# The last quarter of the second token tile's residual sum computed on GpSimd

## The reference, cut to what matters

```python
def rms_norm_2(x, g):
    xf = x.astype(jnp.float32)
    y = xf * lax.rsqrt(jnp.mean(xf * xf, axis=-1, keepdims=True) + RMS_EPS)
    return (y * g.astype(jnp.float32)).astype(x.dtype)

def odd_layer(...):
    ...
    y = jnp.concatenate([y_c, y_d], axis=-1) @ w_out
    return x + rms_norm_2(y, g_post)
```

## Time and profile before

| what | us |
|---|---|
| three runs | 812.29, 813.22, 813.26 |
| their median | 813.22 |
| the profiled execution | 811.32 |
| its span, first to last instruction | 809.6 |
| TensorE busy in it | 798.8 (99%) |
| VectorE busy | 509.2 (63%) |
| ScalarE busy | 478.3 (59%) |
| GpSimd busy | 47.4 (6%) |

### The profile page before, as it was taken

How to read it: one execution, slowest core, us unless ns; L and a number is a source line. 1 busy time by engine, 2 the same in 40 slices (tenths; PEclk the granted TensorE clock), 3 DMA queues, 4 the chain that set the end, 5 groups by cost and what they waited for, 6 DMA issues and landing times.

```text
span 809.6 us, 11514 instructions
## 1 busy us (share of the span) xinstructions
PE 798.8 (99%) x4403; PEld 690.0 (85%) x4403; DVE 509.2 (63%) x770; ACT 478.3 (59%) x766; POOL 47.4 (6%) x79
## 2 busy tenths in 40 slices
PE   7999999999999999999999999999999999999997
PEld 6787888888889999888888789788888898898985
DVE  4666943656566666636456667867574677667553
ACT  5556767563356555535546767337963688566642
POOL 2100000000000000550100102000000010000000
PEclk9999999999999999999999999999999999999999
DMA  7773553755465555696667477435465476376021
GB/s 231 248 234 104 176 155 112 218 181 180 150 208 189 181 182 177 196 235 220 207 188 239 150 220 221 164 123 171 142 229 187 129 229 214 106 210 214 27 96 61
DMA packets 85654, 143.77 MB, mean 178 GB/s; under 512 B 9820, under 2 KB 24145, under 8 KB 85472
## 3 DMA queue, kind: packets, MB, share of 16 engines
q1 hardware_dynamic: 81008, 134.20, 53.0%
q0 software_dynamic: 4384, 8.65, 4.2%
q10 hardware_dynamic: 208, 0.18, 0.1%
HBM read 139.80 MB, written 1.07 MB: 174 GB/s over the span
## 4 chain that ended last, share of the span: by engine, by line
PE 98%; DVE 1%; DMA 1%; ACT 0%; SPq 0%; issue 0%; DVEq 0%
PE acc L1815 24%; PE acc L1816 23%; PE acc L1817 23%; PE acc L1868 5%; PE acc L1871 5%; PE acc L1870 5%; PE aux L1904 2%; PE aux L2189 1%; PE aux L2308 1%; PE aux L2062 1%; PE aux L2134 1%; DMA raw<-in_w_in 1%; PE acc L1846 1%; PE acc L1845 1%; PE acc L1842 1%; PE aux L1968 0%
## 5 line engine op out<-in xcount | busy, mean ns | idle before, releaser
L424 DVE TENSOR_TENSOR wlo<-raw,whi 128x1024 fp32r<-128x1024 f32 (+4 forms) x259 | 303.6, 1194 | 173.5 <-ACT whi L615 171.4
L615 ACT ACTIVATE whi<-raw 128x1024 fp32r<-128x1024 f32 (+4 forms) x259 | 264.0, 1038 | 190.8 <-PE acc L1817 113.1
L1815 PE MATMUL acc<-whi,a_hi 128*128 128x512 f32 (+4 forms) x560 | 212.5, 380 | 4.1 <-DVE wlo L424 4.0
L1817 PE MATMUL acc<-whi,a_lo 128*128 128x512 f32 (+4 forms) x560 | 209.5, 374 | 0.0
L1816 PE MATMUL acc<-wlo,a_hi 128*128 128x512 f32 (+4 forms) x560 | 209.2, 374 | 0.0
L1815 PEld LDWEIGHTS acc<-whi,a_hi 128*128 128x128 f32 x560 | 105.3, 188 | 25.3 <-DVE wlo L424 5.3
L1817 PEld LDWEIGHTS acc<-whi,a_lo 128*128 128x128 f32 x560 | 105.2, 188 | 18.5
L1816 PEld LDWEIGHTS acc<-wlo,a_hi 128*128 128x128 f32 x560 | 105.3, 188 | 17.5
L1868 PE MATMUL acc<-a_hi,whi 128*128 128x256 f32 x320 | 91.1, 285 | 0.0
L1871 PE MATMUL acc<-a_hi,wlo 128*128 128x256 f32 x320 | 90.5, 283 | 0.0
L1870 PE MATMUL acc<-a_lo,whi 128*128 128x256 f32 x320 | 90.5, 283 | 0.0
(11 more groups left out here) (395 smaller groups left out, 887.5 us busy)
## 6 DMA issues: line engine op xcount, KB each, us to landing
raw<-in_even_w_in SPq DMA_DIRECT2D x54, 512.0 KB, 4.5
raw<-in_w_in SPq DMA_DIRECT2D x48, 512.0 KB, 4.3
raw<-in_w_up SPq DMA_DIRECT2D x32, 512.0 KB, 4.5
raw<-in_w_down SPq DMA_DIRECT2D x32, 512.0 KB, 4.7
raw<-in_even_w_out SPq DMA_DIRECT2D x16, 512.0 KB, 4.1
raw<-in_odd_w_in SPq DMA_DIRECT2D x16, 512.0 KB, 4.5
raw<-in_odd_w_out SPq DMA_DIRECT2D x12, 512.0 KB, 4.5
raw<-in_w_branch_gla SPq DMA_DIRECT2D x8, 512.0 KB, 3.5
```

What stands on the lines that cost most here:

```text
L424: return e.tensor_tensor(w_view(wlo[u % SPLIT], u), w_view(raw[u % RAW], u), w_view(whi[u % SPLIT], u).bitcast(F32), ALU.subtract)
L615: act.activation(w_view(whi[u % SPLIT], u), w_view(raw[u % RAW], u), ACT.Copy).then_inc(sem("hi_done"), 1)
L1815: pe.matmul(acc_of(c, t), ah[:, ts], hi[:, k], start=first, stop=False)
L1817: ins = pe.matmul(acc_of(c, t), al[:, ts], hi[:, k], start=False, stop=last)
```

## The change

Tile 1's pieces become 512, 256 and 256 columns. VectorE computes the first two as before. The third, the last quarter, is computed by GpSimd in two steps: `YTMP2 * yrms` in place, then, after it waited for that, the sum with `H`. So that GpSimd knows that `YTMP2` is complete, VectorE issues a `memset` of one column of a spare constant ahead of its two pieces, which counts up `y_ready`. SP's last store waits for GpSimd's `last_piece` in place of VectorE's fifth `h_out`. ScalarE's store stays and is of 256 columns in place of 320.

```diff
-        OUT_PARTS = ((slice(0, 512), slice(512, 1024)), (slice(0, 512), slice(512, 832), slice(832, 1024)))
+        OUT_PARTS = ((slice(0, 512), slice(512, 1024)), (slice(0, 512), slice(512, 768), slice(768, 1024)))
...
-                    sp.wait_ge(sem("h_out"), 4 + i + 1)
+                    sp.wait_ge(sem("h_out") if i < 4 else sem("last_piece"), 4 + i + 1 if i < 4 else 1)
                     sp.dma_start(out[0, t * P:(t + 1) * P, cs], H[:, t, cs]).then_inc(sem("stored"), 16)
...
+                cs = OUT_PARTS[1][2]
+                pool.wait_ge(sem("y_ready"), 1)
+                pool.wait_ge(sem("y_rstd"), 4)
+                chain(pool.tensor_scalar(YTMP2[:, 1, cs], YTMP2[:, 1, cs], yrms[:, 1, 1:2], None, ALU.mult))
+                pool.tensor_tensor(H[:, 1, cs], YTMP2[:, 1, cs], H[:, 1, cs], ALU.add).then_inc(sem("last_piece"), 1)
...
-                    for cs in OUT_PARTS[t]:
+                    if t == 1:
+                        dve.memset(epsc[:, 3:4], 0.0).then_inc(sem("y_ready"), 1)
+                    for cs in OUT_PARTS[t][0:2]:
```

## The result

The change made the kernel slower: 816.47 us (median of 6 runs, 813.96 to 816.97) against 812.62 us (6 runs, 812.01 to 813.26) for the kernel before. The ratio is 1.0038, with a 95% interval of 1.0028 to 1.0049, which is 2.3 to 4.0 us; the two medians are 3.85 us apart, at the upper end of that. Among the six runs after, the three with a mean granted clock of 0.992 took 816.46 to 816.97 us and the two with 0.997 took 813.96 and 814.96. I had forecast 813.7 and "same"; the measured time lies above my range of 812.2 to 814.9.

A forecast was written before the change was run, and what follows sets the result against it. It took TensorE (98% of the chain) as the bound, with only the tail movable. Memset, held scaling, wait, sum and store moved the last landing from 809.16 to 809.65; 813.22 + 0.49 = 813.71 us, range 812.2 to 814.9.

The forecast's parts named there:

- The step that failed: At the program's end: SP, waiting for GpSimd's last piece, holds up nobody; no added time was counted.
- The floor: Tile 1's stores: the memset delays the first store, so the end is 0.10 us later however fast GpSimd is.
- GpSimd's part: Tile 1's last quarter: scaling 0.40 us unhindered, wait 0.23, sum 0.63; held by VectorE, it ends at 807.96.
- GpSimd gets in between: Tile 1's sums: GpSimd's scaling goes before VectorE's second sum; 0.21 us later than before, 813.4; chance 0.28.
- the forecast: Tile 1's sums: VectorE goes first, holding GpSimd's scaling until 806.84; 0.49 us later than before, 813.7; chance 0.40.
- The exclusion: Tile 1's sums: GpSimd stands still during VectorE's two-SBUF-input instruction; 0.26 us is left afterwards for 256 columns.
- The wait for its own result: Between GpSimd's scaling and its sum: a wait of 0.23 us.
- The slack of the last store: Tile 1's last store before the change: queued behind the two others, so its issue has 0.44 us of slack.
- The slow rival: GpSimd's two new instructions: arithmetic much slower than masks, over 0.2% slower from k = 2.7; chance 0.06.

The follow-up runs named there:

- the run on tile 0: Kernel before, with GpSimd's two instructions on tile 0's last quarter and VectorE's first 768 columns of tile 0 in one sum: 812.59 us, ratio 0.9996.
- the wait alone: Changed kernel, but GpSimd only waits at its end and computes nothing; VectorE does all three pieces of tile 1: 814.0 us against 812.71, ratio 1.0017.
- the smaller first piece: Kernel before, with tile 1's pieces 256, 384 and 384 columns instead of 512, 320 and 192, all on VectorE: 812.75 us against 813.15, ratio 0.9998.
- the run with the tiny memset: Kernel where GpSimd only waits at its end, plus a one-column GpSimd memset behind that wait: 815.24 us, ratio 1.0031.

## Why the prediction was wrong, step by step

**The step that failed** is the sentence "SP, which waits for `last_piece` with nothing behind it but the wait for all stores, holds up nobody", together with a part of the change that I did not cost at all: what stands *behind* GpSimd's new instructions on its own engine. I had asked who waits for GpSimd's piece, but not what GpSimd still had to do after it. Its drain stood there, a row of 11.6 us in the trace of before, at a line (64) that I read only as the name of a gap in VectorE's chain. My sum kept the 0.44 us from the last landing to the end of the span; they measured 3.2, because the drain ends 4.7 us behind GpSimd's sum. With the DMA issues drained earlier the same kernel is at 812.79. My words "the prediction fails altogether if anything ahead of the last matmul moves" looked in the wrong direction: what moved lay behind.

**The floor** (0.10 us for the memset, all bytes in 1.51 us) was not what bound. The first sum starts 805.88 - 804.28 = 1.60 us after the last matmul, 1.57 before, so the memset cost about 0.03, less than the 0.10 that I took. I had read that price from two sums 0.45 us apart with a memset between the earlier trace rows, but the same trace has such a gap without one, ahead of the sum at 732.22, which, like the one behind the memset, waits for the sum ahead of it:

```profile
731.77 0.42 DVE L1664 TENSOR_TENSOR ZT<-XN,trig 128x256 f32<-128x256 f32 x1
732.22 0.43 DVE L1665 TENSOR_TENSOR XN<-ZT 128x256 f32<-128x256 f32 x1
```

The bytes moved at the rate of before: 384 KB from about 807.49 to 808.61, and after a gap the last 128 KB from 809.10 to 809.5. Their first byte came 0.83 us after the issue, as in the sum.

**GpSimd's part** came out right in sum and wrong in its terms. From the last matmul to the end of its sum I had 807.96 - 804.02 = 3.94 us; it was 808.24 - 804.28 = 3.96. But:

- The scaling alone is 0.93 us, not the 0.40 of the mask of the same size. A mask was a poor stand-in for a multiply with a per-partition factor.
- It was held by VectorE's first sum only, not by both. That sum ended at 806.63, and the scaling 0.80 us later, at 807.43, just as in the run on tile 0, where no second sum followed. So GpSimd went next (its 0.80 us are the 0.93 less 0.13, as the masks ended 0.26 and 0.49 us after VectorE, 0.14 less than their 0.40 and 0.63). VectorE's second sum paid for it: 0.70 us in place of 0.48 for the same 256 columns in the run in which GpSimd only waits.

```profile
L1788 DVE SCALAR_TENSOR_TENSOR H<-KN,yrms,H 128x256 f32<-128x256 f32 x1 | 0.7, 700 | 0.0
```

```profile
L1786 DVE SCALAR_TENSOR_TENSOR H<-KN,yrms,H 128x256 f32<-128x256 f32 x2 | 0.9, 480 | 0.0
```

The first of these rows is of the changed kernel, the second of the wait alone. This is the rival "GpSimd gets in between", which I had below the forecast. The exclusion itself, which I read from two rows of masks and for which I named the Trainium skill (SBUF — State Buffer, Who interferes with whom), is borne out for the first sum by 1.38 and 1.65 us against 0.93 alone. Its "the other fully blocks" is more than the rows show for the second: that one lost 0.22 us, while the scaling went on for 0.80 us after the first sum.

- The wait for its own result cost 0.09 us (807.43 to 807.52), not the 0.23 of the earlier trace rows. The sum took 0.72 us, between my bounds of 0.40 and 0.80; I took 0.63.

The two mistakes on the scaling, too short and held too long, cancelled.

**The slack of the last store** was right. I had named 1.7 us to landing, in place of 2.0, as its test; it is 1.7. And the smaller first piece shortened the tail by 0.09 us without an earlier last sum.

**The slow rival** (arithmetic 2.7 times the masks' or more) did not come about: 2.3 times for the scaling, 1.1 times my assumption for the sum. The kernel became slower by over 0.2% through something that was on no list.

What stays open: why the hidden drains take 10.5 to 11.6 us when they are reached right behind the loads, where the issues alone would make 4.6. The loads were still under way then. In the five traces with such a drain it ended 2.3 to 2.4 us behind the landing of the last load issued ahead of it (before: 656.78 + 8.3 = 665.08, and 655.88 + 11.57 = 667.45), which fits a drain that waits for the transfers; no experiment varied this. And it stays open what part of the later last matmul in the run with the tiny memset is the kernel's.

## What to carry to other kernels

When an engine that had finished early gets a late instruction, everything that stands behind it at the end of its program becomes late as well: look up its drain at the end of the block, how long it is and what it stands behind, before costing the instruction itself. If GpSimd has issued many DMAs and must do something at the end, put an explicit drain where it is idle. And before shortening the last step of a tail, read whether the last store waits for that step or for the transfers ahead of it.

## What the runs showed of the hardware

- GpSimd's drain took 0.082 us for each DMA that it had issued since its last drain: 0.84, 0.92, 1.26 and 5.43 us for 0, 1, 5 and 56 issues, each with the 0.72 us of a sum in front.
- Reached while its loads were under way, the drain took 10.5 to 11.6 us and ended 2.3 to 2.4 us after the last of them had landed (five traces).
- GpSimd needed 0.93 us for 256 columns times a per-partition factor and 0.72 us for a sum of two tensors of 256 columns, where VectorE did both in one instruction of 0.48 us.
- A store's time to landing here was 0.83 us to the first byte, the time of its bytes (128 KB in 0.38 us), and 0.45 us: 2.0 us for 256 KB, 1.7 us for 128 KB.
